# Channel normalisation moved from its own stage into the branch merge, and matmul operands moved by 64 bytes

## The reference

```python
def conv_branch(u_glu, u_gate, conv_w, conv_b, ln_g, ln_b, w_proj):
    a = u_glu[..., :D_CONV] * jax.nn.sigmoid(u_glu[..., D_CONV:])
    a = depthwise_conv(a, conv_w, conv_b)              # 31 taps
    a = jax.nn.silu(layer_norm(a, ln_g, ln_b))         # over 512 channels
    return (a * jax.nn.silu(u_gate)) @ w_proj

def merge_branches(...):
    y_a = conv_branch(a_glu, a_gate, conv_w, conv_b, cln_g, cln_b, w_proj_a)
    y_b = (o_na * jax.nn.silu(n_gate)) @ w_proj_b      # neighbourhood attention
    y_c = (o_wa * jax.nn.silu(w_gate)) @ w_proj_c      # window attention
    y = sigmoid(g_a) * y_a + sigmoid(g_b) * y_b + sigmoid(g_c) * y_c
    return y @ w_o
```

## The kernel before

| tile | before | after |
|---|---|---|
| `w_hi`, `w_lo` | 0 (128) | 0 (128) |
| `x_hi`, `x_lo` | 0 (128) | 64 (192) |
| `op_hi`, `op_lo` | 0 (128) | 64 (192) |
| `h_hi`, `h_lo` | 64 (64) | 64 (192) |
| `qa` | 64 (64) | 64 (192) |
| `qc` | 96 (224) | 64 (192) |
| `both` (compression, stationary) | 0 (0) | 64 (192) |
| `c_both` (ada, stationary) | 0 (128) | 0 (0) |

## Time and profile before

### The profile page before, as it was taken

The page is one execution under the profiler, slowest core; times in us unless marked ns, Lnnn a source line. Parts: engine busy times, 40 slices in busy tenths (PEclk is TensorE's granted clock), DMA queues, the critical chain, the costliest instruction groups (busy, mean ns, idle before and its releaser), DMA issues. The chain is left out here.

```text
span 2632.5 us, 46562 instructions
## 1 busy us (share of the span) xinstructions
PE 2443.8 (93%) x17814; PEld 2216.6 (84%) x17814; DVE 1507.7 (57%) x2664; ACT 1261.4 (48%) x1978; POOL 232.3 (9%) x228
## 2 busy tenths in 40 slices
PE   6898799999989899999989999999999989998998
PEld 5677568887778689999977789899899878898998
DVE  4489663334558665655456566555555556565554
ACT  5354663332547564434356454543543555555434
POOL 0013000000003100022000000121021000000220
PEclk9899899999989999999999999999999989999999
DMA  8331022232542134554543234455355442343553
GB/s 325 117 108 65 19 98 100 87 111 80 204 162 99 31 129 177 176 192 176 191 144 113 97 129 151 154 180 189 143 190 185 151 145 96 113 145 136 184 178 109
DMA packets 59959, 367.18 MB, mean 139 GB/s; under 512 B 5872, under 2 KB 17184, under 8 KB 17312
## 3 DMA queue, kind: packets, MB, share of 16 engines
q1 hardware_dynamic: 59664, 365.07, 38.8%
q10 hardware_dynamic: 144, 0.01, 0.0%
HBM read 357.68 MB, written 7.37 MB: 139 GB/s over the span
## 5 line engine op out<-in xcount | busy, mean ns | idle before, releaser
L252 PE MATMUL psum<-x_hi,w_hi 128*128 128x256 f32 (+1 forms) x3456 | 1067.9, 309 | 59.2 <-DVE x_lo L606 21.9
L210 DVE TENSOR_TENSOR w_lo<-ring,w_hi 128x1024 fp32r<-128x1024 f32 x652 | 822.9, 1297 | 496.8 <-ACT w_hi L198 496.7
L253 PE MATMUL psum<-x_lo,w_hi 128*128 128x256 f32 (+1 forms) x3456 | 1049.7, 304 | 0.0
L254 PE MATMUL psum<-x_hi,w_lo 128*128 128x256 f32 (+1 forms) x3456 | 1049.2, 304 | 0.0
L198 ACT ACTIVATE w_hi<-ring 128x1024 fp32r<-128x1024 f32 (+1 forms) x652 | 657.8, 1050 | 300.8 <-PE psum L1580 135.5
L252 PEld LDWEIGHTS psum<-x_hi,w_hi 128*128 128x128 f32 x3456 | 670.4, 194 | 103.0 <-issue 63.0
L253 PEld LDWEIGHTS psum<-x_lo,w_hi 128*128 128x128 f32 x3456 | 670.7, 194 | 25.0 <-issue 1.9
L254 PEld LDWEIGHTS psum<-x_hi,w_lo 128*128 128x128 f32 x3456 | 670.1, 194 | 23.4
L1577 PE MATMUL psum<-h_hi,w_hi 128*128 (+1 forms) x640 | 176.7, 276 | 0.0
L1579 PE MATMUL psum<-h_lo,w_hi 128*128 (+1 forms) x640 | 176.7, 276 | 0.0
L1580 PE MATMUL psum<-h_hi,w_lo 128*128 (+1 forms) x640 | 176.7, 276 | 0.0
(11 more groups left out here) (298 smaller groups left out, 3065.1 us busy)
## 6 DMA issues: line engine op xcount, KB each, us to landing
ring<-wstream SPq DMA_DIRECT2D x327, 1024.0 KB, 4.8
kept_hi<-x_hi SPq DMA_DIRECT2D x1, 2048.0 KB, 6.3
kept_lo<-x_lo SPq DMA_DIRECT2D x1, 2048.0 KB, 12.7
x_hi<-kept_hi SPq DMA_DIRECT2D x1, 2048.0 KB, 8.4
x_lo<-kept_lo SPq DMA_DIRECT2D x1, 2048.0 KB, 12.9
rel_bias<-bias_by_distance SPq DMA_DIRECT2D x2, 1024.0 KB, 7.3
na_bias<-rpb SPq DMA_DIRECT2D x4, 438.0 KB, 6.0
cst<-consts SPq DMA_DIRECT2D x1, 1662.0 KB, 11.8
```

Of the source, the lines that this page charges most:

```text
L210: dve.tensor_tensor(w_lo[:, c % 2, h], ring[:, (c + 2 * i) % RING, h], w_hi[:, c % 2, h].bitcast(F32), ALU.subtract).then_inc(split_done.s ...
L252: pe.matmul(o, w_hi[:, c, w_cols], hi, start=first, stop=False)
L253: pe.matmul(o, w_hi[:, c, w_cols], lo, start=False, stop=False)
L254: return pe.matmul(o, w_lo[:, c, w_cols], hi, start=False, stop=last)
```

## The change

1. Four padding tiles (64 or 32 bytes) move `x_hi`/`x_lo`, `op_hi`/`op_lo`, `both` and block 2's tiles on the right side of SBUF, as the table above shows.
2. `conv_norm_stage` is gone. The attention's bias is made in `glu_stage`: flips of four heads behind GLU chunks 0 and 2, the mask by VectorE in steps 1 and 3. In layer 0 it lies in `x`, which is fetched again from HBM during the merge. The two sums, centring, squares, root, scaling and SiLU of the convolution are steps 1 to 6 of `merge_stage`, whose branches now come in the order near, window, convolution (the weight stream too); the squares are in `y`.
3. The convolution's taps are dealt over the first nine steps of `qkv_stage`, by the width of each chunk.
4. nk and nq are not split; near attention reads them in fp32, as window attention does. `x_hi` and `x_lo` stay where they are, so the four copies to HBM and back go, and transposed probabilities have a tile of their own.

```diff
+        sb("half_line", [P, HALF_LINE])
         x_hi = sb("x_hi", [P, KT, 2 * S], F32R)
         x_lo = sb("x_lo", [P, KT, 2 * S], F32R)
+        sb("half_line", [P, HALF_LINE])
+        sb("quarter_line", [P, HALF_LINE // 2], side="right")
...
+            conv, squares = branches[2], y[:, 0:4, 0:tok]
+            gains, biases = par(layer, "cln_g"), par(layer, "cln_b")
+            b0, c0, q0, r0, s0, f0 = step.n, centred.n, squared.n, rooted.n, scaled_x.n, affine.n
+
+            def sums(e):
+                a = 2048 * ((g0[0] + e) % 2) + 1024
+                return psum[:, a:a + tok]
+
             with nc.Block() as block:
                 @block.sync
                 def _(sp):
+                    if layer == 0:
+                        sp.dma_start(x[:, :, 0:S], xT).then_inc(stored.sem, 16)
+                        sp.dma_start(x[:, :, S:2 * S], ctxT).then_inc(stored.sem, 16)
...
+                    def sum_tiles(e, tile, ready=None):
+                        for k in range(4):
+                            if ready:
+                                ready(k)
+                            mm = pe.matmul(sums(e), const("ones_conv"), tile(k), start=k == 0, stop=k == 3)
+                        mm.then_inc(step.sem, 1)
+
                     for j, (kind, b, i) in enumerate(seq):
+                        if j == 1:
+                            sum_tiles(0, lambda k: conv[:, k, 0:tok])
+                        elif j == 4:
+                            sum_tiles(3, lambda k: squares[:, k, :], lambda k: pe.wait_ge(squared.sem, q0 + k + 1))
+                            pe.wait_ge(centred.sem, c0 + 4)
+                        elif j == 7:
+                            pe.wait_ge(rooted.sem, r0 + 1)
...
+                        if j == 2:
+                            for k in range(4):
+                                act.wait_ge(centred.sem, c0 + k + 1)
+                                act.activation(squares[:, k, :], conv[:, k, 0:tok], ACT.Square).then_inc(squared.sem, 1)
+                        elif j == 4:
+                            act.wait_ge(step.sem, b0 + 2)
+                            inverse_root(act, sums(3), rs[:, 0:tok], eps_col, r0)
+                        elif j == 6:
+                            for k in range(4):
+                                act.wait_ge(scaled_x.sem, s0 + k + 1)
+                                act.activation(conv[:, k, 0:tok], conv[:, k, 0:tok], ACT.Silu, scale=gains[:, k:k + 1],
+                                               bias=biases[:, k:k + 1]).then_inc(affine.sem, 1)
...
+                            if b == 2:
+                                dve.wait_ge(affine.sem, f0 + 2 * i + 2)
...
+                        if j == 1:
+                            dve.wait_ge(step.sem, b0 + 1)
+                            for k in range(4):
+                                dve.tensor_tensor(conv[:, k, 0:tok], conv[:, k, 0:tok], sums(0), ALU.subtract
+                                                  ).then_inc(centred.sem, 1)
+                        elif j == 5:
+                            dve.wait_ge(rooted.sem, r0 + 2)
+                            for k in range(4):
+                                dve.tensor_tensor(conv[:, k, 0:tok], conv[:, k, 0:tok], rs[:, 0:tok], ALU.mult
+                                                  ).then_inc(scaled_x.sem, 1)
...
+                        na_bias = x[:].rearrange("p k t -> p (k t)")[:, 0:NA_COLS + 256]
+                    else:
+                        na_bias = sb("na_bias", [P, NA_COLS + 256], stack=st5, side="right")[:]
...
+                    sb("half_line", [P, HALF_LINE], stack=st2)
...
+                        if layer == 0 and i == 0:
+                            dve.wait_ge(stored.sem, stored.n + 32)
...
-                    merge_stage((conv_out, nq, wq), y, sg, prod, op_hi, op_lo, tok, take_out,
+                    merge_stage(layer, (nq, wq, conv_out), y, sg, prod, op_hi, op_lo, tok, take_out,
...
+                    for a in range(2):
+                        off = (layer * HEADS * 15 + 5 - a) * 31 + 15 - (GRID_W - 1)
+                        sp.dma_start(na_bias[a * GRID_W:(a + 1) * GRID_W, raw:].rearrange("p (h r) -> p h r", h=HEADS),
+                                     bass.AP(rpb.tensor, off, [[1, GRID_W], [15 * 31, HEADS], [1, RUN]])
+                                     ).then_inc(loaded.sem, 16)
...
+                        if j % 2 == 0:
+                            pe.wait_ge(loaded.sem, lb + 32)
+                            for h in range(2 * j, 2 * j + 4):
+                                if h >= 4:
+                                    pe.wait_ge(hpart.sem, p0 + h - 3)
+                                rows = bass.AP(na_bias.tensor, na_bias.offset + raw + h * RUN,
+                                               [list(na_bias.ap[0]), [31, 6], [1, GRID_W]])
+                                mm = pe.matmul(psum[:, bank[h]:bank[h] + 6 * GRID_W], const("flip_rows"), rows,
+                                               start=True, stop=True)
+                            mm.then_inc(parted.sem, 1)
...
+                        if j % 2:
+                            dve.wait_ge(parted.sem, f0 + j // 2 + 1)
+                            for h in range(2 * j - 2, 2 * j + 2):
+                                o = na_bias[:, 6 * GRID_W * h:6 * GRID_W * (h + 1)]
+                                dve.tensor_tensor(
+                                    o.rearrange("p (e c) -> p e c", c=GRID_W),
+                                    psum[:, bank[h]:bank[h] + 6 * GRID_W].rearrange("p (e c) -> p e c", c=GRID_W),
+                                    const("na_mask").unsqueeze(1).to_broadcast([P, 6, GRID_W]), ALU.add
+                                    ).then_inc(hpart.sem, 1)
+                    dve.memset(na_bias[:, NA_COLS:], 0.0)
...
-            cuts = [round(len(taps) * j / n) for j in range(n + 1)]
+            share = [0] + [t // S for _, t, _ in plan[:-1]]
+            cuts = [round(len(taps) * sum(share[:j + 1]) / sum(share)) for j in range(n)] + [len(taps)]
...
-                    sp.dma_start(kept_hi[:, :, 0:tok], x_hi[:, :, 0:tok].bitcast(F32)).then_inc(stored.sem, 16)
-                    sp.dma_start(kept_lo[:, :, 0:tok], x_lo[:, :, 0:tok].bitcast(F32)).then_inc(stored.sem, 16)
                     load_ahead(sp, n)
-                    sp.wait_ge(stored.sem, stored.n + 32)
...
-        def conv_norm_stage(layer, tok, src, scratch, na_bias, jobs):
...
-                near = steps_of(tok, (x_hi[:, 4:8, :], x_lo[:, 4:8, :]), (x_hi[:, 0:4, :], x_lo[:, 0:4, :]), 2,
-                                lambda h, t: nv[:, t, h * DH:h * DH + DH],
-                                lambda h, qt: before_zeros(na_bias[:], (6 * h + 2 - 2 * qt) * GRID_W, NA_COLS),
-                                None, 0)
+                near = steps_of(tok, (nq,), (nk,), 2, lambda h, t: nv[:, t, h * DH:h * DH + DH],
+                                lambda h, qt: before_zeros(na_bias, (6 * h + 2 - 2 * qt) * GRID_W, NA_COLS), None, 0)
...
-                              attention_buffers(st, 2 * S, spent[:].rearrange("p (a b) t -> p a b t", b=2)))
+                              attention_buffers(st, 2 * S))
-                    @block.sync
-                    def _(sp):
-                        sp.wait_ge(scored.sem, a.at(scored, len(near) - 1))
-                        sp.dma_start(x_hi[:, :, 0:tok].bitcast(F32), kept_hi[:, :, 0:tok]).then_inc(stored.sem, 16)
-                        sp.dma_start(x_lo[:, :, 0:tok].bitcast(F32), kept_lo[:, :, 0:tok]).then_inc(stored.sem, 16)
-                        sp.wait_ge(stored.sem, stored.n + 32)
...
+            sb("half_line", [P, HALF_LINE], stack=st)
...
-        for b, (gate, proj) in enumerate(((A_GATE, "w_proj_a"), (N_GATE, "w_proj_b"), (W_GATE, "w_proj_c"))):
+        for b, (gate, proj) in zip((1, 2, 0), ((N_GATE, "w_proj_b"), (W_GATE, "w_proj_c"), (A_GATE, "w_proj_a"))):
```

More of the change, by code:

```diff
@@ L97 @@
     ("k_w2", 2 * 128), ("v_w2", 2 * 64)])
+HALF_LINE = 16
 class Count:
@@ L815, in attention_buffers, with merge_stage @@
                     *(sb(name, [P, 3, 2], stack=st, side=side) for name in ("mx", "den", "fac", "neg")))
-        def merge_stage(branches, y, sg, prod, op_hi, op_lo, tok, take_out, halves):
+        def merge_stage(layer, branches, y, sg, prod, op_hi, op_lo, tok, take_out, halves):
             seq = []
@@ L961, in _ @@
                         x_lower(dve, OUT_CHUNKS - 1)
+            step.n += 2
+            rooted.n += 2
+            for c in (centred, squared, scaled_x, affine):
+                c.n += 4
             parted.n += 6
@@ L989, in block1 @@
             with ExitStack() as st:
-                conv_out = sb("conv_out", [P, 4, 2 * S], stack=st)
-                nq = sb("nq", [P, 4, 2 * S], stack=st)
-                wq = sb("wq", [P, 4, 2 * S], stack=st)
-                def scratch_of_x(k):
-                    return (nq, wq)[k // 4][:, k % 4, :]
-                with ExitStack() as st2:
```

(23 more changed lines are left out.)

138 lines of the change are left out of this document (26 added, 112 removed).

## The result

| | before | after |
|---|---|---|
| median of 4 runs, us | 2634.76 | 2607.97 |
| profiled execution: span, us | 2632.5 | 2599.7 |
| `x` 256 columns wide, mean distance, ns | 119.9 | 116.9 |
| `h`, 256 columns | 113.4 | 116.7 |
| `x`, 512 columns | 226.9 | 229.0 |

The ratio is 0.9899, 95% interval 0.9884 to 0.9914: 27 us faster, where 88 were forecast. The time lies 23 us above the range's upper end of 2585. (The distances are start to start, at full clock, means over all matmuls of the kind without a wait behind them.) One entry of the table of addresses has to be put right: after the change `op_hi` begins at byte 210240 in layer 0 and 197952 in layer 1, which is 64 modulo 256, not 192. All other entries modulo 256 stand as they are there.

A forecast was written before the change was run, and what follows sets the result against it. TensorE, busy for 93% of the span, was taken as the bound; -70 us (operand places), -18.1 (block 1) and 0 (taps) make -88 from 2634.85, forecast 2547 us, range 2528 to 2585.

The forecast's parts named there:

- part 1: Padding puts matmul operands 64 bytes off the weights' 128-byte lines: 6.8 ns gained each, 81.2 us, of which 70 counted.
- the wrong 64: Rival on operand places: period is 256 bytes and only residue 64 is quick; level, or 2714 us; chance 0.03.
- The price for 512 columns: Gain per moved 512-column matmul: no row showed it; lower end 0, upper 13.3 ns, 6.8 taken.
- Part 2: Block 1 without its norm stage: -45.3 us removed, +10.4, +10.3, +4.4 and +2.1 us added, sum -18.1 us.
- flips, masks and sums: Costs added in block 1: bias flips +10.4 us, mask additions with memset +4.4 us, sums over channels +10.3 us.
- Part 3: Convolution's taps dealt over nine chunks of the projections, none after the last: 0 us, bounds -6 and +6.
- The address is not the cause: Rival on operand places: moving them gives nothing, only block 1's 18 us are left; 2617 us; chance 0.10.
- Block 1 gives nothing: Rival: projection chunks on TensorE wait 2 us each for their split, so 18 us are gone; 2565 us; chance 0.07.
- all of the excess goes: Rival: everything moved, h too, runs at 109 ns instead of 113.2, 56 us more; 2500 us; chance 0.04.

The follow-up runs named there:

- e4: The changed kernel plus a last stage where TensorE alone runs matmuls with weights and moving operand at various residues, 256 or 512 columns; no kernel time given.
- e5: The probe stage of e4 with more entries, five times each, varying what runs ahead of a run of matmuls; no kernel time given.
- e7: e6 plus two triples of 256-column matmuls on the weights themselves ahead of ten stretches of 256 columns; 2577.26 us, ratio 0.9797.
- e1: The changed kernel without its padding tiles, so block 1's change alone; 2618.42 us, ratio 0.9931.
- e8: e6 with the convolution's taps dealt evenly over all ten steps, as in the kernel before; 2580.66 us, ratio 0.9792.
- e6: e3 with layer 0's 512-column operands at the weights' residue, 128 modulo 256, and 256-column operands staying at 64; 2576.90 us, ratio 0.9775.
- e3: The changed kernel with larger pads, putting x, op, h, qa, qc and both at 64 modulo 256; 2589.49 us, ratio 0.9824.
- e10: The probe stage of e4 with other matmul widths, and with w_lo at a residue of its own; no kernel time given.
- e2: The kernel before with the change's padding tiles alone; 2625.93 us, ratio 0.9962.
- e9: The kernel before with the operand places of e6 alone, block 1 keeping its norm stage; 2603.30 us, ratio 0.9885.

## Why the prediction was wrong

**The bound was read rightly.** TensorE sets the pace, and it does so by what stands between the starts. The paces that it read come back in the probe: 120.0 and 226.7 ns at a difference of 0, 113.3 at -64.

**The step that failed is part 1:** "Each gains 120.0 - 113.2 = 6.8 ns." Measured, `x` of 256 columns gained 2.9 ns and not 6.8, and `h`, costed at nothing, lost 3.3. Three things were wrong in it.

- *The distance was taken modulo 128.* `h_hi` lay 64 below the weights' residue, `x_hi` was put 64 above. e4 has 113.3 on the one side and 117.8 on the other. The table of addresses had both residues; the prediction named the risk ("the wrong 64") and gave it 3 in 100, on the ground that the distance to the weights is the same either way round. It is 64 both ways, but modulo 256 the sign counts.
- *A pace was taken for a property of the place.* On both sides 113.3 and 117.8 occur, and what runs ahead has a part in which of them (e4, e5, e7). `h` stood at 113.3 in the kernel before and came from `x` at 120.0, as the pairs 128 and 64 of e4 do; after the change `h` lies at `x`'s own place and goes on at `x`'s pace, 117.8 in three of the four feed-forwards and 113.3 in the last. A pace is carried on within one place; from place to place it isn't by rule: `op` of 256 columns, at -64 behind `x` at +64, had 113.3 in two of its six chunks, one of them directly behind `x` at 117.8, and 117.8 in four.
- *The price for 512 columns had its lower end at 0.* It was a loss: 2.1 ns for `x` at +64, 6.4 for `op` at -64 (after the change against e1), where a gain of 6.8 was taken.

In numbers, after the change against e1, each kind's count by the difference of its mean distance: `x` of 256 columns 8870 x -2.9 = -25.7 us, `op` of 256 -1.0, `h` 2112 x 3.3 = +7.0, `qa` +0.4, `qc` -0.4, `x` of 512 1670 x 2.1 = +3.5, `op` of 512 +1.8. Sum -14.4; the spans of these two executions differ by 2599.7 - 2616.7 = -17.0, the medians by -10.4 (the profiled execution after the change was the quickest of its four, that of e1 among the slowest of its five). Forecast: -70.

**Part 2 was right:** -18.1 forecast, -15.8 by e1's medians and -18.2 by its ratio. Its terms: layer 0's attention starts 17.7 us sooner where -23.8 + 5.2 + 2.2 = -16.4 stood; flips, masks and sums took the durations of the earlier trace rows. One term was too large: near attention in fp32 was to cost 2.1 us. Layer 0's merge began at 376.17 in the kernel before:

```profile
376.17 0.47 PE L252 MATMUL psum<-x_hi,w_hi 128*128 128x512 f32 x1 [1.22 <-PEq L1421]
```

So from attention's start to it 376.17 - 285.40 = 90.8 us passed before, and 358.60 - 267.70 = 90.9 after: the fp32 products cost nothing that can be seen. That they hide behind the softmax is likely and not shown. **Part 3**, 0 within 6 us, was right too: attention starts 1.5 us sooner than in e8, and the medians of e6 and e8 can't be told apart.

**The rivals.** "The address is not the cause" forecast 2617 and came nearest to 2608, for a wrong reason: e3 and e6 move nothing but addresses and are worth 19 and 31 us. "The wrong 64" had the period of 256 bytes, though not its prices: it wanted `x` unchanged and `h` back at 120.0. "Block 1 gives nothing" falls by e1's 16 us, and for "all of the excess goes" no run has anything under 113.3 ns at 256 columns. The Trainium skill's rule that stood against part 1 ("TensorE: Matmul & The Clock Gate", "Step-by-step: what each phase is for": stream and weight load read through independent ports, and the load takes nothing from the running matmul) does not agree with the distances at 256 columns here, where the load's residue alone moves the pace (e10: 120.0 to 118 ns); at 192, 224 and 320 columns no run speaks against it. Whether the ports are the reason no run shows.

**Still open:** why the distance to the weights counts at all, why -64 is quicker at 256 columns and slower at 512, what picks the pace behind a wait, and what is carried from one place to the next. The runs show outcomes only.

## What to carry to other kernels

When TensorE is full, divide the time of a long row of matmuls at full clock by its number of starts and compare with columns / 2.4 GHz; a constant excess is a reason to look at the places of weights and moving operand, and the difference has to be kept with its sign and modulo 256, for each width apart. One place that is quick in one stage is not evidence for the same price elsewhere: a probe stage at the end of the kernel, with a wait ahead of each run and pairs without one, would have shown all of part 1's errors. And two stages on the same tiles can differ by 4% (113.3 and 117.8 ns). The executions of e3 lay between 2579 and 2594 us; whether the paces make that difference is not shown, since one execution of each kernel left a trace.

## What the runs showed of the hardware that was not expected

- Matmuls on the same tiles at the same addresses run at 113.3 or at 117.8 ns and stay so: after the change `x` and then `h`, at one place, from 1656.7 to 1841.2 us. In the traces of the change and of e2, e3 and e6 to e9 none of the stretches of more than 60 matmuls on one operand without a wait (23 to 26 in each trace) changes its pace.
- Two triples of matmuls at difference 0 (0.72 us) of 256 columns led to 113.3 at difference -64 in five of five runs behind 117.8 and five of five behind a wait (e5), and in all ten stretches of e7, six of which had 113.3 already. Twenty-four matmuls of 512 columns at difference 0 led to 117.8 at -64 in five of five (e5).
- Shorter is not quicker below 256 columns: 192 and 224 columns start every 111.5 ns or so, though 224 columns are 93.3 ns at 2.4 GHz. From 320 on (146.7, 173.3, 226.7) the excess over the columns is 13.3 ns at the quickest place (e10, e4).
